# RWKV time mix: the 16-column inverse fed through a DRAM buffer instead of constant products, two units in one walk

## The chip, the cores and the metric

One core of a Trainium2 chip runs the whole program in one launch. The metric is the device time in microseconds, from a few executions of the same program; less is better. TensorE runs its matmuls in fp32 here; VectorE, ScalarE and the DMA queues of SyncE, ScalarE and GpSimd work beside it, held in order by semaphores.

## The reference

The model has four layers of width 1024 over 256 tokens, batch 1. Each layer is FFN, mixer, FFN. The mixers are RWKV-7 time mix, Mamba-2, sliding attention and RWKV-7 again; then one more block with a recurrent unit and attention follows. The change is inside the two RWKV-7 time mixes only:

```python
def step(state, inp):
    r_t, w_t, k_t, v_t, kk_t, a_t = inp
    sa = einsum('bhvk,bhk->bhv', state, -kk_t)
    state = state * w_t + sa[..., None] * (kk_t * a_t) + v_t[..., None] * k_t
    return state, einsum('bhvk,bhk->bhv', state, r_t)
```

The kernel does not step through tokens. It takes chunks of 128 tokens and writes the recurrence as products of matrices. For that, each head and chunk needs the inverse of a unit lower triangular 128x128 matrix, 1 + L, where L comes from products of the scaled `a` and `kk` (the "near" products). The inverse starts with its 16x16 diagonal blocks, which are found column by column (the "walk"), and is then grown to 32, 64 and 128 by products.

## The kernel before

There are 16 heads, laid out two to a tile of 128 partitions (eight tiles), and two chunks. A unit is one chunk (`b`) of eight heads (`hf`), `u = 2 b + hf`, so there are `UNITS = 4` units; `i` is the head's half of the partitions. `j` is 0 or 1 for the first and second RWKV sublayer (`n = 1` and `n = 10`).

TensorE's order is written out by hand in `rw_products`. It projects key tiles k0 to k7 (with the low ranks between), r0 to r7, v0 to v7, for `j = 1` the low rank v1, then g1 (two tiles), and then the second steps v2 and g2. A tile is eight products of 128x128 weights with 256 columns of a mix, into one of three PSUM banks in turn (`RING = 3`); a tile may begin when ScalarE has evacuated the tile three before it. Weights come in slots of 24 blocks (1.5 MB), three slots resident; SyncE's queue refills a slot when TensorE is done with it. The function `beside` of a tile is called after its fourth and its eighth product: there `near(u, i)` and `spread(u, i)` are placed, in r3 to r7 and v0 to v6.

The path of one unit before the change, for each half `i`: four near products (64 rows of contraction) of TensorE go to bank 3. VectorE (`base` in `rw_vector`) multiplies them with the constant `near`, which keeps the 16x16 diagonal blocks above the diagonal (L2344), sums over the eight blocks to 64 columns (L2349), and expands them with `same_row` to 1024 columns (L2352). TensorE multiplies this with the constant `same16` (`spread`, two products of 512 columns), which copies each row of a block to all of its 16 partitions, in banks 4 to 7. Then the walk: 15 pairs of VectorE instructions, a product (L2364, reading the PSUM) and a subtraction (L2365), on 8 heads and 15, 14, ... 1 columns, each waiting for the one before. The result is in `wkv_base`, read later by `open_y` (L2428). So VectorE walks four times a stage; between them it does the mixes of v and g (L2235), the bonus (L2376), `scaled_both` (L2382, L2383) and, for `j = 0`, the streamed sum of the conditioning weights (`beside`, L521: one 768 KB chunk `ada_in`, whose buffer GpSimd's queue then refills).

ScalarE (`rw_act`) evacuates every tile in TensorE's order (L2095), stores `v_first` for `j = 0` (L2133) and loads it for `j = 1` (L2137), and reads the second steps only when `scaled_both` is done (`rw_keys`). The low rank tiles v1 and g1 go to `lora`, in the arena from 8 K words on.

## Time and profile before

| what | us |
|---|---|
| three executions | 3020.34, 3021.47, 3025.54 |
| median | 3021.47 |
| span of the profiled execution, first to last instruction | 3017.6 |
| around the span, against the median | 3.9 |

The page of the profile gives for the span the busy time of each engine, a row of 40 slices, the DMA queues, the chain that ended last, the costliest groups by line, and the DMA issues. TensorE's granted clock is full in nearly all of the span (mean 0.992). No time of its own is recorded for the profiled execution beside its span, so the sums below are made against the span and carried over to the median. The timelines list merged instructions in order, with the idle time of the engine before one and what released it. An fp32 product shows as two or more records of TensorE.

### The profile page before, as it was taken

To read this page: it belongs to the slowest core of one execution; us is meant where nothing else is said; L and a number is where in the kernel's file an instruction comes from. 1 tells how busy PE (TensorE), PEld (TensorE's weight loads), DVE (VectorE), ACT (ScalarE), POOL (GpSimd) and SP (SyncE) were. 2 spreads that over 40 slices of the span, in tenths; PEclk is the share of its full clock that TensorE was granted. 3 is DMA by queue.
4 is the path that set the end of the run, shared out by engine and by line. 5 is a ranking of instruction groups with operands and counts; after the bars stand their busy time and mean duration, and the time that the engine had idled before them with its cause. 6 is when DMAs were issued, how large, how long until landed. Compare 5 with 4: busy or idle time off the path is not lost. (4 is left out here: it accounts for less than half of the span.)

```text
span 3017.6 us, 50256 instructions
## 1 busy us (share of the span) xinstructions
PE 2933.6 (97%) x20094; PEld 2574.1 (85%) x20094; DVE 2351.2 (78%) x3516; ACT 1392.3 (46%) x2260; POOL 97.2 (3%) x187
## 2 busy tenths in 40 slices
PE   7999999999999999999999999999999999999998
PEld 6887788888889888888886888887788888989887
DVE  6988877998878857888867888887865866665785
ACT  4534123555545734555444555544123544465553
POOL 0000000000000000000000000000000000000000
PEclk9999999999999999999999999999999999999999
DMA  8683436686666337666764666672303553444453
GB/s 354 256 318 147 153 105 238 249 319 229 241 241 231 112 120 271 231 256 248 270 250 157 236 253 265 237 276 84 119 23 115 200 188 127 168 149 148 171 190 133
DMA packets 69675, 609.33 MB, mean 202 GB/s; under 512 B 7728, under 2 KB 7888, under 8 KB 31824
## 3 DMA queue, kind: packets, MB, share of 16 engines
q1 hardware_dynamic: 42768, 459.36, 40.9%
q0 software_dynamic: 26352, 144.74, 12.8%
q8 instruction: 160, 2.62, 0.3%
q10 hardware_dynamic: 336, 2.13, 0.2%
q14 instruction: 59, 0.48, 0.0%
HBM read 604.10 MB, written 2.10 MB: 201 GB/s over the span
## 5 line engine op out<-in xcount | busy, mean ns | idle before, releaser
L1073 ACT ACTIVATE unit_high<-weights 128x1024 fp32r<-128x1024 f32 x576 | 609.6, 1060 | 624.9 <-PE psum L1142 335.3
L1084 DVE TENSOR_TENSOR unit_low<-weights,unit_high 128x1024 fp32r<-128x1024 f32 x576 | 703.1, 1222 | 146.9 <-ACT unit_high L1073 146.6
L1138 PE MATMUL psum<-h_part,unit_high 128*128 128x512 f32 x3024 | 769.2, 393 | 5.0 <-DVE h_part L995 5.0
L1138 PEld LDWEIGHTS psum<-h_part,unit_high 128*128 128x128 f32 x3024 | 542.0, 189 | 105.0 <-DVE h_part L995 5.5
L1142 PEld LDWEIGHTS psum<-h_part,unit_low 128*128 128x128 f32 x3024 | 416.6, 190 | 31.0
L1142 PE MATMUL psum<-h_part,unit_low 128*128 128x256 f32 x3024 | 432.3, 282 | 0.0
L331 PE MATMUL psum<-in_part,w_part 128*128 128x256 f32 x2784 | 359.4, 288 | 11.6 <-DVE in_part L999 5.8
L331 PEld LDWEIGHTS psum<-in_part,w_part 128*128 128x128 f32 x2784 | 344.7, 194 | 29.5 <-issue 15.0
L1159 PE MATMUL psum<-hidden,unit_high 128*128 128x512 f32 x1386 | 348.3, 392 | 0.0
L521 DVE SCALAR_TENSOR_TENSOR ada_sum<-ada_in,c_act,ada_sum 128x1536 f32<-128x1536 f32 x154 | 278.7, 1812 | 28.9 <-DMA ada_in<-in_ada_w 28.8
L1279 DVE TENSOR_REDUCE arena<-psum 128x256 f32<-128x512 f32 x378 | 259.9, 687 | 49.2 <-PE psum L1142 38.6
L1159 PEld LDWEIGHTS psum<-hidden,unit_high 128*128 128x128 f32 x1386 | 248.8, 189 | 44.0
L331 PE MATMUL psum<-arena,weights 128*128 128x256 f32 (+4 forms) x1360 | 270.3, 370 | 6.2 <-DVE arena L2235 4.4
L331 PEld LDWEIGHTS psum<-arena,weights 128*128 128x128 f32 (+3 forms) x1360 | 214.5, 188 | 59.0 <-issue 28.0
L1437 DVE TENSOR_TENSOR w_part<-weights,w_part 128x1024 fp32r<-128x1024 f32 x144 | 175.1, 1220 | 86.4 <-ACT w_part L1431 85.4
L1166 PEld LDWEIGHTS psum<-hidden,unit_low 128*128 128x128 f32 x1584 | 214.5, 191 | 13.3
L1166 PE MATMUL psum<-hidden,unit_low 128*128 128x256 f32 x1584 | 221.1, 282 | 0.0
L331 PE MATMUL psum<-arena 64*64 64x64 f32 (+5 forms) x2752 | 182.5, 250 | 4.1 <-DVE arena L2959 2.3
L331 PEld LDWEIGHTS psum<-arena 64*64 64x64 f32 (+3 forms) x2752 | 150.2, 148 | 31.9 <-issue 16.9
L1431 ACT ACTIVATE w_part<-weights 128x1024 fp32r<-128x1024 f32 x144 | 150.8, 1050 | 16.0 <-PE psum L331 16.0
L1244 ACT ACTIVATE hidden<-arena 128x256 fp32r<-128x256 f32 x198 | 82.9, 419 | 111.8 <-DVE arena L1346 91.0
L505 POOL DMA_DIRECT2D ada_in<-in_ada_w x130 | 68.7, 528 | 1431.2 <-DVE ada_sum L521 1090.0
(332 smaller groups left out, 2861.4 us busy)
## 6 DMA issues: line engine op xcount, KB each, us to landing
weights<-in_weights SPq DMA_DIRECT2D x290, 1536.0 KB, 6.5
ada_in<-in_ada_w POOLq DMA_DIRECT2D x182, 768.0 KB, 5.9
consts<-in_consts POOLq DMA_DIRECT2D x1, 1556.0 KB, 12.2
x<-in_x SPq DMA_DIRECT2D x1, 1024.0 KB, 8.8
v_first<-arena ACTq DMA_DIRECT2D x1, 1024.0 KB, 5.3
arena<-v_first ACTq DMA_DIRECT2D x1, 1024.0 KB, 4.8
weights<-in_weights SPq DMA_DIRECT2D x1, 512.0 KB, 5.5
out<-x SPq DMA_DIRECT2D x1, 512.0 KB, 2.7
```

Of the source, the lines that this page charges most:

```text
L331: ins = self.k.nc.tensor.matmul(out, lhsT=w, rhs=x, start=start, stop=stop, is_transpose=turn)
L521: ins = k.nc.vector.scalar_tensor_tensor(out, buf, c, out, ALU.mult, ALU.add)
L1073: k.nc.scalar.activation(k.unit_part[0][:, n % UNIT_RING], w, ACT.Copy).then_inc(k.sem["unit_high"], 1)
L1084: k.nc.vector.tensor_tensor(k.unit_part[1][:, n % UNIT_RING], w, k.unit_part[0][:, n % UNIT_RING].bitcast(FP32), ALU.subtract).then_inc(k. ...
L1138: mm(k.psum[:, 2 * (j % 2) + half, :].rearrange("p (i t) -> p i t", i=2), lhsT=part(2 * j + half, 0, t), rhs=k.h_parts[:, :, t], start=t = ...
L1142: ins = mm(k.psum[:, 2 * (j % 2) + half, 0:T], lhsT=part(2 * j + half, 1, t), rhs=k.h_part[0][:, t], start=False, stop=t == KT - 1, skip_g ...
L1159: mm(k.psum[:, out_bank(d), :].rearrange("p (i t) -> p i t", i=2), lhsT=w, rhs=x, start=f == 0, stop=f == FT - 1, skip_group_check=True)
L1166: ins = mm(k.psum[:, out_bank(d), 0:T], lhsT=part(UNITS_UP + v, 1, b), rhs=k.hidden_part[f][:, 0], start=False, stop=f == FT - 1, skip_gro ...
L1244: k.nc.scalar.activation(k.hidden_part[j][:, 0], k.hidden[:, j % RING], ACT.Copy)\
L1279: v.tensor_reduce(to[:, j % RING], k.psum[:, 2 * (j % 2) + half, :].rearrange("p (i t) -> p t i", i=2), AX.X, ALU.add).then_inc(k.sem["gat ...
L1431: self.k.nc.scalar.activation(self.k.w_part[0][:, m % RING], w, ACT.Copy).then_inc(self.k.sem["w_high"], 1)
L1437: self.k.nc.vector.tensor_tensor(self.k.w_part[1][:, m % RING], self.weights(m)[1], self.k.w_part[0][:, m % RING].bitcast(FP32), ALU.subtr ...
```

## The change

The 16x16 blocks are no longer spread by a product. `near(u)` issues the near products of both halves in one go, alternating between them, into two banks of 4 to 7; near(0) and near(1) stand within r3, near(2) and near(3) within r4. ScalarE copies only the 32x32 diagonal squares (`near_read`), VectorE picks of each the 16 columns that belong to the partition (`choose`, two instructions with the constant `halves16`). ScalarE's queue writes two units of that, 128 KB, to the DRAM buffer `near_rows` (`near_out`), and reads it back so that each partition holds all 16 rows of its block (`low_in`: two transfers of 1 MB a pair of units, each row of 8 KB going to 16 partitions) to the arena at 8 K and at 27 K words. The second place is the buffer `raw`, which was a tensor of its own and is now the arena's end, so that one access pattern with a step of 19 K words reaches both. The walk then takes two units at once, reading these instead of the PSUM. The first place is also that of `lora`, so ScalarE waits for the second walk before it reads v1 and g1. Its second `low_in` stands after the evacuation of v0 and waits for the first walk. The waits of TensorE on `wk_base` go.

```diff
-        self.step = k.small[:, 192:312]
+        self.step = k.small[:, 192:432]
-        self.spread = cut(26, 1024).rearrange("p (n s t) -> p n s t", n=4, s=16)
+        self.near_q = [cut(26 + i / 4, 256).rearrange("p (m t) -> p m t", m=8) for i in range(2)]
+        self.near_t = cut(26.5, 512).rearrange("p (u m t) -> p u m t", u=UNITS, m=8)
+    def low(k, at, *steps):
+        pitch = 27 * 1024 + KT * (T + 1)
+        return bass.AP(tensor=k.arena, offset=8 * 1024 + at, ap=[[pitch, P], *steps])
+    def low_rows(k, i):
+        pitch = 27 * 1024 + KT * (T + 1)
+        return bass.AP(tensor=k.arena, offset=(8, 27)[i] * 1024, ap=[[pitch, P], [1, 2048]])
...
-    def spread(u, i):
-        pe.wait_ge(s["wk_expanded"], 2 * UNITS * j + 2 * u + i + 1)
-        if u and i == 0:
-            pe.wait_ge(s["wk_base"], UNITS * j + u)
-        for h in range(2):
-            mm(k.psum[:, (6, 4)[i] + h, :], k.const("same16"),
-               z.spread[:, 2 * h:2 * h + 2].rearrange("p n s t -> p (n s t)"), True, True,
-               s["wk_spread"] if h else None)
+    def near(u):
+        b, hf = divmod(u, 2)
+        pe.wait_ge(s["rw_keys"], 3 * j + 1 + b)
+        if b:
+            pe.wait_ge(s["wk_near_read"], UNITS * j + u - 1)
+        for p in range(4):
+            for i in range(2):
+                mm(k.psum[:, 5 + 2 * hf - i, p * P:(p + 1) * P], z.a[z.rows(i), 4 * hf + p, z.now(b)],
+                   z.kk[z.rows(i), 4 * hf + p, z.now(b)], True, True, s["wk_near"] if p == 3 and i else None)
...
         if at == (3, 0):
-            near(0, 0)
-        if at == (3, 1):
-            near(0, 1)
+            near(0)
+            near(1)
         if at == (4, 0):
-            spread(0, 0)
...
+            near(2)
+            near(3)
...
+    def near_read(u):
+        act.wait_ge(s["wk_near"], 2 * UNITS * j + u + 1)
+        if u >= 2:
+            act.wait_ge(s["near_chosen"], UNITS * j + u - 1)
+        for g in range(4):
+            part = slice(32 * g, 32 * g + 32)
+            ps = k.psum[part, 4 + 2 * (u % 2):6 + 2 * (u % 2), :].rearrange("p i (n c) -> p i n c", n=4)
+            ins = act_(z.near_q[u % 2][part].rearrange("p (i n) c -> p i n c", i=2), ps[:, :, :, part], f.Copy)
+        ins.then_inc(s["wk_near_read"], 1)
+    def near_out(b):
+        act.wait_ge(s["near_chosen"], UNITS * j + 2 * b + 2)
+        act.dma_start(near_rows[2 * b:2 * b + 2].rearrange("u p x -> p u x"), z.near_t[:, 2 * b:2 * b + 2].rearrange("p u m t -> p u (m t)"))\
+            .then_inc(s["near_out"], 16)
+    def low_in(b):
+        if b:
+            act.wait_ge(s["wk_base"], 2 * j + 1)
+        act.wait_ge(s["near_out"], 16 * (2 * j + b + 1))
+        for i in range(2):
+            rows = near_rows[2 * b + i].rearrange("(c s) x -> c (s x)", s=16)
+            act.dma_start(z.low_rows(k, i), rows.unsqueeze(1).to_broadcast([8, 16, 16 * P])).then_inc(s["low_in"], 16)
...
+        if m == 3:
+            near_read(0)
+            near_read(1)
         evacuate("r", m, z.r[:, m], f.Copy)
+        if m == 3:
+            near_out(0)
+            near_read(2)
+            near_read(3)
+        if m == 4:
+            low_in(0)
+        if m == 5:
+            near_out(1)
     act.wait_ge(s["rw_keys"], 3 * j + 1)
     for m in range(KT):
         evacuate("v", m, z.v[:, m], f.Copy)
+        if m == 0:
+            low_in(1)
+    act.wait_ge(s["wk_base"], 2 * j + 2)
...
+    def choose(u):
+        dve.wait_ge(s["wk_near_read"], UNITS * j + u + 1)
+        even, odd = (k.const("halves16")[:, i:i + 1] for i in range(2))
+        q = z.near_q[u % 2]
+        own.of(v.tensor_scalar(z.near_t[:, u], q[:, :, 0:16], even, None, mult))
+        v.scalar_tensor_tensor(z.near_t[:, u], q[:, :, 16:32], odd, z.near_t[:, u], mult, add)\
+            .then_inc(s["near_chosen"], 1)
+
+    def base(b):
+        x = z.base[:, 2 * b:2 * b + 2]
+        own.of(v.tensor_copy(x.rearrange("p u m t -> p (u m) t"),
+                             k.const("same_row").unsqueeze(1).to_broadcast([P, 16, 16])))
+        dve.wait_ge(s["low_in"], 32 * (2 * j + b + 1))
         for c in range(15):
             w = 15 - c
-            step = z.step[:, 0:8 * w].rearrange("p (m c) -> p m c", m=8)
-            own.of(v.tensor_tensor(step, low[:, :, c, c + 1:16], x[:, :, c:c + 1].to_broadcast([P, 8, w]), mult))
-            own.of(v.tensor_tensor(x[:, :, c + 1:16], x[:, :, c + 1:16], step, sub))
+            step = z.step[:, 0:16 * w].rearrange("p (u m c) -> p u m c", u=2, m=8)
+            low = z.low(k, c * P + c + 1, [19 * 1024, 2], [16, 8], [1, w])
+            own.of(v.tensor_tensor(step, low, x[:, :, :, c:c + 1].to_broadcast([P, 2, 8, w]), mult))
+            own.of(v.tensor_tensor(x[:, :, :, c + 1:16], x[:, :, :, c + 1:16], step, sub))
...
-    base(0, value_mixes, lambda: None)
-    base(1, lambda: None, gate_mixes)
-    base(2, beside, bonus)
-    base(3, beside, scaled_both)
+    choose(0)
+    choose(1)
+    value_mixes()
+    choose(2)
+    choose(3)
+    beside(2)
+    base(0)
+    gate_mixes()
+    bonus()
     beside()
+    base(1)
+    scaled_both()
```

## Rows read from the trace of the kernel before

**Rows 1.** The page, part 1: busy us, share of the span, instructions.

```profile
PE 2933.6 (97%) x20094; PEld 2574.1 (85%) x20094; DVE 2351.2 (78%) x3516; ACT 1392.3 (46%) x2260; POOL 97.2 (3%) x187
```

**Rows 2.** Busy time by stretch: us, PE, PEld, DVE, ACT, POOL, clock, DMA share, GB/s.

```profile
291.40:369.50 78.10, 75.11 (x329) 56.92 (x328) 68.73 (x181) 7.03 (x16) 1.06 (x2) 1.00 0.35 129
2102.70:2182.20 79.50, 78.04 (x345) 60.12 (x344) 65.50 (x180) 7.41 (x17) 0.00 (x0) 1.00 0.31 115
```

**Rows 3.** Timeline of TensorE, stage A: start us, us, engine line op, [idle before <-releaser].

```profile
291.43 1.16 PE L331 MATMUL psum<-arena 64*128 64x128 f32 x8
292.51 1.99 PE L331 MATMUL psum<-arena,weights 128*128 128x256 f32 x8
...
301.47 1.88 PE L331 MATMUL psum<-arena,consts 128*128 128x512 f32 x4
303.18 1.89 PE L331 MATMUL psum<-arena,weights 128*128 128x256 f32 x8
...
369.51 5.21 PE L331 MATMUL psum<-arena,weights 128*128 128x256 f32 x32 [0.47 <-ACT arena L2095]
```

**Rows 4.** Timeline of TensorE, stage B.

```profile
2102.75 1.16 PE L331 MATMUL psum<-arena 64*128 64x128 f32 x8
...
2182.24 3.71 PE L331 MATMUL psum<-arena,weights 32*128 32x256 f32 x32 [0.47 <-ACT arena L2095]
...
2189.38 1.16 PE L331 MATMUL psum<-arena 64*128 64x128 f32 x16
2190.47 3.72 PE L331 MATMUL psum<-arena,consts 128*128 128x256 f32 x16
```

**Rows 5.** Timeline of VectorE, stage A.

```profile
303.45 0.28 DVE L2364 TENSOR_TENSOR small<-psum,wkv_base 128x120 f32<-128x120 f32 x1 [2.08 <-PE psum L331]
303.77 0.28 DVE L2365 TENSOR_TENSOR wkv_base<-wkv_base,small 128x120 f32<-128x120 f32 x1
...
311.01 0.17 DVE L2365 TENSOR_TENSOR wkv_base<-wkv_base,small 128x8 f32<-128x8 f32 x1
311.22 0.15 DVE L2366 COPY small<-consts 128x1 f32<-128x1 f32 x1
311.29 0.68 DVE L2344 TENSOR_TENSOR arena<-psum,consts 128x512 f32<-128x512 f32 x1
...
314.20 0.68 DVE L2344 TENSOR_TENSOR arena<-psum,consts 128x512 f32<-128x512 f32 x1
...
337.61 3.25 DVE L2376 SCALAR_TENSOR_TENSOR arena<-arena,params 128x256 f32<-128x256 f32 x8
...
358.82 2.28 DVE L2383 TENSOR_TENSOR arena<-arena 128x2048 f32<-128x2048 f32 x1
...
369.06 1.82 DVE L521 SCALAR_TENSOR_TENSOR ada_sum<-ada_in,c_act,ada_sum 128x1536 f32<-128x1536 f32 x1
```

**Rows 6.** Timeline of ScalarE, stage A.

```profile
308.12 0.38 ACT L2095 ACTIVATE arena<-psum 128x256 f32<-128x256 f32 x1 [6.07 <-PE psum L331]
311.57 0.38 ACT L2095 ACTIVATE arena<-psum 128x256 f32<-128x256 f32 x1 [3.07 <-PE psum L331]
...
362.96 1.28 ACT L2095 ACT_TABLE_LOAD   x1 [0.41 <-ACT arena L2095]
...
372.23 1.21 ACT L2095 ACTIVATE arena<-psum 128x256 f32<-128x256 f32 x4 [2.77 <-PE psum L331]
```

**Rows 7.** The page, part 6: DMA issues, KB each, median us to landing.

```profile
out<-x SPq DMA_DIRECT2D x1, 512.0 KB, 2.7
```

**Rows 8.** DMA issues of the stretch 2100 to 2185 us.

```profile
weights<-in_weights SPq DMA_DIRECT2D x5, 1536.0 KB, 6.2
arena<-v_first ACTq DMA_DIRECT2D x1, 1024.0 KB, 4.8
```

**Rows 9.** Busy time by stretch, two slices of stage A.

```profile
303.30:305.40 2.10, 2.10 (x12) 1.61 (x11) 1.74 (x7) 0.00 (x0) 0.00 (x0) 1.00 0.50 80
...
307.50:309.60 2.10, 2.10 (x11) 1.87 (x10) 1.79 (x10) 0.38 (x1) 0.00 (x0) 1.00 0.85 363
```

More of the change, by code:

```diff
@@ L216, in const_parts @@
         "head_ones": same,
-        "same16": row // 16 == col // 16,
-        "near": (row // 16 == col // 16) & (row < col),
+        "halves16": row[:, 0:1] // 16 % 2 == np.arange(2)[None, :],
         "same_row": row % 16 == np.arange(16)[None, :],
@@ L423, in layout @@
     k.wkv_base = sb("wkv_base", [P, 512])
[L424 removed]
+    k.raw = k.arena[:, 27 * 1024:].rearrange("p (n t) -> p n t", n=KT)
     k.raw_bias = k.small[:, 488:490]
@@ L451, in layout @@
               "rw_turned_read", "rw_gated", "v_first_moved",
-              "wk_near", "wk_expanded", "wk_spread", "wk_base", "wk_am", "wk_open", "wk_y",
+              "wk_near", "near_chosen", "near_out", "low_in", "wk_base", "wk_am", "wk_open", "wk_y",
               "wk_x_read", "wk_lx", "wk_t", "wk_x32", "wk_x32_read", "wk_y32",
@@ L1782, in rw_products @@
     for m in range(KT):
-        tile("v", m, 4, beside_v)
+        tile("v", m, 4)
     if j:
@@ L1795, in rw_products @@
     evacuated("g1", 1)
-    pe.wait_ge(s["wk_near_read"], 2 * UNITS * (j + 1))
+    pe.wait_ge(s["wk_near_read"], UNITS * (j + 1))
     for i in range(2):
@@ L2081, in norm_bank, with rw_act @@
     return 5 if n == 0 or n < NORMS and SUBS[n - 1] != "ffn" else 3
-def rw_act(k, act, ev, j, v_first):
+def rw_act(k, act, ev, j, v_first, near_rows):
     s, z, f, tiles = k.sem, RwTiles(k), ACT, RwOrder(j, ev.q)
@@ L2165, in at, with near_again_read @@
         act.wait_ge(s[name], c.count(step, steps))
-    def near_read(c):
-        act.wait_ge(s["wk_near"], 3 * UNITS * j + 2 * UNITS + c.u + 1)
+    def near_again_read(c):
+        act.wait_ge(s["wk_near"], 2 * UNITS * j + UNITS + c.u + 1)
         act_(z.am[c.hf], c.pair(0), f.Copy).then_inc(s["wk_am"], 1)
@@ L2209, in rw_act @@
         if n < UNITS:
-            near_read(units[n])
+            near_again_read(units[n])
         if n >= 2:
@@ L2284, in rw_vector @@
         mod_columns(k, dve, own, n + 1)
-    v.tensor_scalar(z.one_less_ka, k.param(f"rw_k_a{j}", 0, KT), -1.0, 1.0, mult, add).then_inc(s["rw_one_less"], 1)
+    own.mark(v.tensor_scalar(z.one_less_ka, k.param(f"rw_k_a{j}", 0, KT), -1.0, 1.0, mult, add))
     beside(2)
@@ L2293, in scaled_key @@
         return v.tensor_tensor(z.k[:, t], z.k[:, t], z.k_factor[:, t], mult)
-    dve.wait_ge(s["rw_one_less"], j + 1)
+    own.wait()
     for t in range(KT):
@@ L2339, in value_mixes @@
             mix(4, t)
-    def base(u, lead, between):
-        for i in range(2):
-            dve.wait_ge(s["wk_near"], 3 * UNITS * j + 2 * u + i + 1)
-            v.tensor_tensor(z.near, k.psum[:, 3, :].rearrange("p (n t) -> p n t", n=4),
-                            k.const("near").unsqueeze(1).to_broadcast([P, 4, P]), mult).then_inc(s["wk_near_read"], 1)
-            if i == 0:
-                lead()
-            dve.wait_ge(s["wk_near_read"], 2 * UNITS * j + 2 * u + i + 1)
-            own.of(v.tensor_reduce(z.near_t, z.near.rearrange("p n (c t) -> p n t c", t=16), AX.X, add))
-            if i:
-                dve.wait_ge(s["wk_spread"], 2 * UNITS * j + 2 * u + 1)
-            v.tensor_tensor(z.spread, z.near_t.unsqueeze(2).to_broadcast([P, 4, 16, 16]),
-                            k.const("same_row").unsqueeze(1).unsqueeze(3).to_broadcast([P, 4, 16, 16]), mult)\
-                .then_inc(s["wk_expanded"], 1)
-        x = z.base[:, u]
-        own.mark(v.tensor_copy(x, k.const("same_row").unsqueeze(1).to_broadcast([P, 8, 16])))
-        between()
-        own.wait()
-        dve.wait_ge(s["wk_spread"], 2 * UNITS * j + 2 * u + 2)
-        low = k.acc.rearrange("p t (s c) -> p t s c", s=16)
@@ L3856, in build @@
     v_first = nc.dram_tensor("v_first", (P, KT, T), FP32, kind="Internal").ap()
+    near_rows = nc.dram_tensor("near_rows", (UNITS, P, P), FP32, kind="Internal").ap()
     with ctx:
@@ L3898, in _ @@
                 elif kind == "rwkv":
-                    rw_act(k, act, ev, n, v_first)
+                    rw_act(k, act, ev, n, v_first, near_rows)
                 elif kind == "mamba":
```

49 lines of the change are left out of this document (4 added, 45 removed).

## The prediction

> **What bounds the kernel now.** I read the busy shares first: TensorE is busy for 97% of the span, no other engine for more than 78% [rows 1]. So the question for any edit is what it does to TensorE's order, and for work that leaves TensorE the question is who becomes late instead. The change sits in two stages, the "r", "v" and "g1" projections of the two RWKV sublayers. Their windows are 291.4 to 369.5 and 2102.7 to 2182.2 us, and TensorE is busy for 75 of 78 and 78 of 80 us there at full clock, with VectorE at 69 and 66 [rows 2]. I call the first stage A and the second B. In TensorE's own timeline [rows 3, 4] the reader sees three kinds of work in turn: projections (sixteen records a tile), a near product (8 records, 64 rows) and a spread (4 records, 512 columns). TensorE is idle for 3.0 us of A and 1.5 of B in all, 0.47 of it right before "g2" [rows 2 to 4]. So it carries these stages; VectorE is nearly as full, and starts what follows its last walk at 369.06, half a microsecond before "g2" [rows 3, 5]. Outside them both orders stay, and behind them TensorE is again the busy engine, so I take time saved there as kept.
>
> **Part 1, the spread goes.** Each stage has 8 spreads (4 units, two halves). From the start of one to the start of the next work is 303.18 - 301.47 = 1.71 us [rows 3]. 8 x 1.71 = 13.7 us a stage.
>
> **Part 2, near products by pairs.** Now 8 groups of 8 records at 1.08 us (292.51 - 291.43) [rows 3]. The new loop alternates the two 64-row halves, which is how the near products are taken again later: 16 records in 2190.47 - 2189.38 = 1.09 us [rows 4]. So four groups of 1.09 instead of eight of 1.08: 4.3 us less a stage.
>
> **TensorE's new stage.** A tile of sixteen records takes 3.45 us (ScalarE's evacuations at 308.12 and 311.57) [rows 6]. A holds 14.5 tiles from 291.43 on (half of r3, r4 to r7, eight v, two g1), B one more (v1). A: 14.5 x 3.45 = 50.0, near 4.4, two changes to 64 rows and back 0.4, last wait 0.5, together 55.3 instead of 369.51 - 291.43 = 78.1: 22.8 less. B: 15.5 x 3.45 = 53.5 + 5.3 = 58.8 instead of 79.5: 20.7 less. Parts 1 and 2 are 18.0 of it; the rest are the waits on VectorE and some changes between shapes. If nothing else is late, 43.5 us go, and "g2" starts at 346.7 and 2161.5.
>
> **Part 3, VectorE.** Masking, reducing and expanding go (one half takes 314.20 - 311.29 = 2.9 us, 8 a stage: 23 us), replaced by eight products of 128 columns. A product of 120 columns takes 0.28 us [rows 5]; I take 0.3, some 2.4 us. One walk takes 311.22 - 303.45 = 7.8 us. A step of 120 columns takes 0.28 us and one of 8 takes 0.17, which is 1 ns a column [rows 5]; the doubled walk adds 2 x 960 columns = 2.0 us, so 9.8 us for two units instead of 15.5. Its operand now comes from SBUF with a stride; L2364 (from PSUM) and L2365 (SBUF only) both take 0.28 us, so I charge nothing for that, and up to 5.8 us (two separate walks) as the other bound. The Trainium skill's page VectorE: DVE Perf Modes, section on the TRN2 errata, has a table in which a PSUM source costs 62 cycles more than an SBUF source. By it, an estimate, each walk's fifteen reads would be 1 us shorter; the two lines of the walk show no such difference. VectorE is then free for more than half of the stage, so it isn't the bound by its own work.
>
> **Part 4, ScalarE.** Sixteen copies of 256 columns on 32 partitions a stage, by the copies of 128x256: 0.38 alone, 0.30 in a row of four [rows 6], so 1.2 to 1.5 us a unit, hidden: ScalarE is busy for 7 us of the stage [rows 2]. What isn't hidden is its order. The low_in of block 1 waits for walk 0 (the buffers are reused), and behind it on ScalarE stand the evacuations of v1 to v7. TensorE has three banks, so tile v4 waits for v1. After v7, ScalarE waits for walk 1 before it evacuates g1 (and v1's low rank), and "g2" on TensorE waits for g1.
>
> **Part 5, the way through DRAM: the unknown.** One near_out writes 128 KB. The nearest rows are a store of 512 KB (2.7 us) and a load of 1 MB (4.8) [rows 7, 8]; issued at 296, it lands by 299 or by 301, before ScalarE has done r4 (301.8), so it costs nothing at either end. One low_in is two transfers of 1 MB each on ScalarE's queue. Call its time from issue to landing L. 1 MB in the v_first load takes 4.8 us, a 1.5 MB slot 6.2 [rows 8]; the difference is 2.8 us a MB, leaving 2.0 fixed, and the engines move 363 GB/s at a share of 0.85 [rows 9], 427 at full. At that rate two MB take 4.9 us, so L is at least 6.9, alone and over all engines. But v_first has 128 rows on each side, and low_in's source has eight rows of 8 KB in front, each sent to sixteen partitions. No row here shows how such a transfer is dealt out. If only eight of the sixteen engines get it, the data take 9.8 us and L is 11.8 alone. I take this, as the rows in front are what can be dealt out and the whole megabyte comes from 64 KB of DRAM; that choice is the weakest step. The Trainium skill's page DMA: Bandwidth & Descriptors (section "Why a DMA increments its semaphore by 16 and not by 1") says that the number of engines is the largest up to 16 that divides the slowest dimension of both sides, which is 8 here, and its rules for kernel authors warn of a short outermost dimension. No row of this case shows such a transfer.
>
> Others share those engines. A slot of 1.5 MB is 3.7 us of each engine at that rate, an ada_in of 0.75 MB 1.8. A slot is freed at the start of r5, its data begin some 2 us later (80 GB/s in the slice from 303.3 on [rows 9], where r5 began at 303.18 [rows 3]), and in the new order r5 starts at 301.4, at the moment of low_in 0. The next slot comes with v0, ten us later. In A beside(2) also frees two ada_in at 303 and 305.
>
> **Sum, stage A.** low_in 0 issued 301.8. L = 2.0 + 9.8 + 3.7 (slot) + 3.7 (two ada_in) + 3.7 (next slot) = 22.9, landed 324.7; walk to 334.5. TensorE could start v4 at 325.5; it starts at 335.6 (issue of low_in 1, v1's evacuation). low_in 1 issued 335.2; L = 11.8 + 3.7 + part of one ada_in = 16; gate mixes and bonus (3.25 us each) and one ada product (1.82) [rows 5] hide in it. Walk 351.2 to 361.0. Then v_first's issue, the table load (1.28) and two evacuations [rows 6]: "g2" at 363.5, 6.0 before today. **Stage B** lies 1811.3 later and has no ada_in. low_in 0 issued 2113.1, L = 11.8 + 3.7 + 2.5 = 18, walk ends 2140.9; low_in 1 issued 2141.6, L = 15.5, walk ends 2166.9; "g2" at 2169.8, 12.4 before today. scaled_both (two products of 2.28 us [rows 5]) ends behind the walk but ahead of its users, because TensorE has 5 us of "g2" products first. Together 18.4 us.
>
> **Rivals.** (a) The transfers run over all engines. A: L0 = 2.0 + 4.9 + 3.7 + 3.7 = 14.3, walk to 325.9, v4 at 327.0, 1.5 late; the rest on time. B on time. 43.5 - 1.5 = 42 us: 2979.5. For it: every transfer in the trace with 128 rows in front; against it: the shape. (b) The stalls are heavier than my shares: each L is 2 to 4 us more, or each walk is by a stride that costs as much: 8 to 16 us of the gain, 3011 to 3019. (c) Slower. "g2" in A starts at 324.6 + L0 + L1, so the sign turns at L0 + L1 = 44.9 (45.9 in B), a mean of 22.7. It needs low_in at a quarter of the engines, or slowed by reading the same DRAM row sixteen times: data 19.6 instead of 9.8, four times 9.8 more, 39 - 18 = 21 us slower: 3042. (d) The halved near groups or the merged walk bring less than their rows say, as TensorE's gain is covered by the DRAM path anyway: no change of the result unless (a) holds, then 2984.
>
> **Numbers.** Before: span 3017.6, median of the runs 3021.5, so 3.9 lie around the span and stay. 3021.5 - 18.4 = 3003. Chances: forecast 0.55, (a) with (d) 0.28, (b) 0.12, (c) 0.05. The range runs from 2978 (all 43.5) to 3013 (each L 2.5 us more). Within 0.2% (6 us, about what a measurement of this kernel can tell from no change) is part of (b). Faster 0.88, same 0.07, slower 0.05.
>
> **What would show it.** TensorE: no 512-column products on consts in these windows, near groups of 16 records at 1.09. VectorE: steps of 240 columns at 0.41 us. ScalarE's DMA rows: low_in's time to landing, 12 to 23 us by the forecast, 7 to 14 by (a). TensorE idle before v4 and before "g2", released by ScalarE: 10 and 6 us in A, 5 and 3 in B; under 3 in all by (a). If L is below 12 everywhere, the forecast is wrong by its weakest step. If there is idle time elsewhere, the assumption that saved time is kept is wrong.

## The result and the profile after

| | median of the runs, us | lowest to highest | profiled execution's span | mean granted clock |
|---|---|---|---|---|
| before | 3023.16 (4 runs, one more beside the changed kernel) | 3020.34 to 3025.54 | 3017.6 | 0.992 |
| after | 3061.44 (4 runs) | 3060.17 to 3064.65 | 3060.0 | 0.978 |

The ratio is 1.0133, with a 95% interval of 1.0121 to 1.0145: the changed kernel is 38 us slower. The forecast was 3003, with a range of 2978 to 3013, so the size and the sign were both wrong.

TensorE's timeline of stage A in the changed kernel (start, us, and the idle time before it with its releaser) answers to [rows 3]:

```profile
293.36 2.06 PE L330 MATMUL psum<-arena 64*128 64x128 f32 x32
...
299.00 2.06 PE L330 MATMUL psum<-arena 64*128 64x128 f32 x32
300.98 26.17 PE L330 MATMUL psum<-arena,weights 128*128 128x256 f32 x120
354.21 23.23 PE L330 MATMUL psum<-arena,weights 128*128 128x256 f32 x96 [27.06 <-ACT arena L2061]
395.32 7.32 PE L330 MATMUL psum<-arena,weights 128*128 128x256 f32 x32 [17.88 <-ACT arena L2061]
402.57 1.16 PE L330 MATMUL psum<-arena 64*128 64x128 f32 x16
```

and of stage B, which answers to [rows 4]:

```profile
2132.61 2.06 PE L330 MATMUL psum<-arena 64*128 64x128 f32 x32
...
2140.24 26.17 PE L330 MATMUL psum<-arena,weights 128*128 128x256 f32 x120
2189.27 27.33 PE L330 MATMUL psum<-arena,weights 128*128 128x256 f32 x112 [22.87 <-ACT arena L2061]
2224.51 6.00 PE L330 MATMUL psum<-arena,weights 32*128 32x256 f32 x32 [7.91 <-ACT arena L2061]
```

The order of work is the one forecast: near products in two short groups, no products with a constant, then projections without a gap up to v4. The two stalls stand where the prediction put them, before v4 and before "g2", both released by ScalarE. Only their size is another: 27.1 and 17.9 us in A (10 and 6 forecast), 22.9 and 7.9 in B (5 and 3 forecast). From the first near product to the end of "g2" the stage grew by 26.0 us in A (402.57 - 293.36 = 109.2 us, 83.2 before) and by 14.7 in B. That is 40.7 us, where the runs differ by 38.3 and the two profiled spans by 42.4; ahead of A, between the stages and behind B the spans differ by 2 us or so each, so nothing of size changed there.

Why ScalarE was late is read on VectorE and on ScalarE's queue. These are the first rows of both walks and the issues of low_in in stage A, then VectorE in stage B:

```profile
342.53 0.41 DVE L2361 TENSOR_TENSOR small<-arena,wkv_base 128x240 f32<-128x240 f32 x1 [34.86 <-DMA arena<-near_rows]
382.96 0.41 DVE L2361 TENSOR_TENSOR small<-arena,wkv_base 128x240 f32<-128x240 f32 x1 [22.21 <-DMA arena<-near_rows]
```

```profile
303.02 1.17 ACTq L2088 DMA_DIRECT2D arena<-near_rows  x1
304.23 0.59 ACTq L2088 DMA_DIRECT2D arena<-near_rows  x1
...
352.52 1.21 ACTq L2088 DMA_DIRECT2D arena<-near_rows  x2
353.77 0.94 ACT L2061 ACTIVATE arena<-psum 128x256 f32<-128x256 f32 x3 [36.50 <-issue]
```

```profile
2177.59 0.41 DVE L2361 TENSOR_TENSOR small<-arena,wkv_base 128x240 f32<-128x240 f32 x1 [34.13 <-DMA arena<-near_rows]
2212.11 0.41 DVE L2361 TENSOR_TENSOR small<-arena,wkv_base 128x240 f32<-128x240 f32 x1 [18.02 <-DMA arena<-near_rows]
```

VectorE stood still for the transfer, four times. From the issue to the first step of the walk, L is 342.53 - 303.02 = 39.5 and 382.96 - 352.52 = 30.4 us in A. In B low_in is issued at 2142.27 and 2187.58, so L is 35.3 and 24.5. The forecast had 22.9, 16, 18 and 15.5. The four differences add up to 57.4 us, and the forecast missed by 3061.4 - 3003 = 58.4 (56.7 in the change, 18.4 less forecast and 38.3 more measured). That these come so close is partly chance, since slower records of TensorE, below, add 4.4 us to the stages that no L holds.

Two more views show what the transfer did and suffered. The page's queue of ScalarE (packets, MB, share of 16 engines), and the DMA issues of the stretch 290 to 400 us (KB each, median us to landing):

```profile
q10 hardware_dynamic: 2512, 11.04, 1.3%
```

```profile
weights<-in_weights SPq DMA_DIRECT2D x5, 1536.0 KB, 16.9
...
ada_in<-in_ada_w POOLq DMA_DIRECT2D x3, 768.0 KB, 20.4
```

The queue has 2512 packets, where it had 336. The 2176 more are 8 x 136 for the low_in and 4 x 272 for the stores. 136 is 128 rows of 8 KB and 8 small packets. I read the small ones as one for each engine that took part: eight of the sixteen. A transfer with 128 rows in front has 144 packets, 16 small ones (run 1, below). And a weight slot, which landed in 6.8 us in stage A before (median of the stretch 290 to 370 us) and in 6.2 in B [rows 8], now took a median of 16.9 in A and 14.7 in B. In A without any low_in (run 2) it takes 6.2.

### The profile page after: what moved, and what is told of

It reads as the page before. It is cut to its first block and busy times, and to the rows that moved or that the text cites. A ratio compares the mean times of both kernels' runs of the same rounds, so it can differ in the third digit from the quotient of the medians.

```text
span 3060.0 us, 50004 instructions
## 1 busy us (share of the span) xinstructions
PE 2906.1 (95%) x20030; PEld 2564.7 (84%) x20030; DVE 2292.3 (75%) x3356; ACT 1403.5 (46%) x2292; POOL 97.2 (3%) x187
## 3 DMA queue, kind: packets, MB, share of 16 engines
q10 hardware_dynamic: 2512, 11.04, 1.3%
## 5 line engine op out<-in xcount | busy, mean ns | idle before, releaser
L330 PEld LDWEIGHTS psum<-in_part,w_part 128*128 128x128 f32 x2784 | 345.7, 194 | 30.0 <-issue 15.5
L330 PE MATMUL psum<-arena,weights 128*128 128x256 f32 (+4 forms) x1360 | 276.4, 382 | 80.8 <-ACT arena L2061 76.6
L330 PEld LDWEIGHTS psum<-arena,weights 128*128 128x128 f32 (+3 forms) x1360 | 223.0, 195 | 130.5 <-ACT arena L2061 78.6
L330 PE MATMUL psum<-arena 64*64 64x64 f32 (+5 forms) x2752 | 172.2, 250 | 2.9 <-DVE arena L2963 2.3
L330 PEld LDWEIGHTS psum<-arena 64*64 64x64 f32 (+3 forms) x2752 | 142.3, 148 | 26.5 <-issue 15.6
```

What stands on the lines that cost most here:

```text
L330: ins = self.k.nc.tensor.matmul(out, lhsT=w, rhs=x, start=start, stop=stop, is_transpose=turn)
```

## What was tried, and what each run showed

Three theories of the long L: **E**, the transfer runs on eight engines, as I had taken, and the rest of L is work of other queues beside it; **R**, on top of that the same DRAM row is read sixteen times; **P**, on top of E the destination, sixteen neighbouring partitions for each row in front, slows the packets. Single executions below have no interval; the beginning of stage A alone lay anywhere from 291.4 to 296.8 us between kernels, so differences under 5 us between single runs are not read. The kernel before took 3024.5 and 3025.4 beside the first two groups of runs.

**1. The transfers alone.** No part of the kernel; each transfer of 1 MB is issued when the one before has landed:

```python
("rows128", [[ROW, 128]]), ("eight_repeated", [[ROW, 8], [0, 16]]),
("eight_distinct", [[17 * ROW, 8], [ROW, 16]]), ("sixteen_repeated", [[ROW, 16], [0, 8]]), ("one_row", [[0, 128]])
```

> Leaves out all of the model's computation: it only times transfers of 1 MB (128 rows of 8 KB) from DRAM to SBUF on ScalarE's queue, each alone, each case twice. The changed kernel's low_in took 39 and 30 us in the first stage. Theory E (eight engines, the rest is other traffic): with eight source rows in front, rows repeated or not, 1 MB lands in about 7 us, with 128 or sixteen rows in front in about 4.5, repetition makes no difference, and the pair of low_in alone takes 12, beside a weight slot on SyncE's queue 15. Theory R (the repeated read of one DRAM row is slow): eight distinct is at most 7, but eight repeated, sixteen repeated and one row are far above it, the pair alone at 20 or more.

The start of one issue to the start of the next is the time of a transfer (ScalarE's queue in its timeline):

```profile
7.98 0.35 ACTq L77 DMA_DIRECT2D d_rows<-in_w  x1
12.90 1.16 ACTq L77 DMA_DIRECT2D d_eight_repeated<-in_w  x1
23.67 0.61 ACTq L77 DMA_DIRECT2D d_eight_distinct<-in_w  x1
34.83 0.59 ACTq L77 DMA_DIRECT2D d_sixteen_repeated<-in_w  x1
41.79 0.33 ACTq L77 DMA_DIRECT2D d_one_row<-in_w  x1
46.21 1.23 ACTq L77 DMA_DIRECT2D pair<-near_rows  x2
67.15 0.81 ACTq L77 DMA_DIRECT2D pair<-in_w  x2
74.52 1.21 ACTq L77 DMA_DIRECT2D pair<-near_rows  x2
```

128 rows: 4.9 us. Eight in front: 10.8 with repeated rows and 11.2 with distinct ones. Sixteen in front: 7.0. One single row, read 128 times: 4.4. The pair of low_in with nothing beside it: 67.15 - 46.21 = 20.9, where I had 11.8; a pair of 128-row loads: 7.4. Beside one weight slot the pair took 24.5 us, and 23.1 the second time. R falls: repetition costs nothing. E alone falls too. This is how 128 rows and eight in front move (length, GpSimd's busy time, clock, share of 16 engines, GB/s):

```profile
7.98:12.90 4.92, 0.00 (x0) 1.00 0.61 213
12.90:23.67 10.77, 0.00 (x0) 1.00 0.39 97
```

The share times the length is how long all sixteen engines would be busy with the megabyte. For 128 rows it is 0.61 x 4.92 = 3.0 us; an engine has 8 packets of 8 KB, 0.38 us each. For eight in front it is 0.39 x 10.77 = 4.2 us of sixteen engines, so 8.4 of eight, for 16 packets each, 0.53 us a packet. (The packet counts of the two are 144 and 136.) So the packets themselves are 1.4 times as long, and there are twice as many to an engine.

**2. No low_in at all.** The walk reads the constants instead; nothing waits for DRAM.

```diff
-        for i in range(2):
-            rows = near_rows[2 * b + i].rearrange("(c s) x -> c (s x)", s=16)
-            act.dma_start(z.low_rows(k, i), ...).then_inc(s["low_in"], 16)
...
-        dve.wait_ge(s["low_in"], 32 * (2 * j + b + 1))
...
-            low = z.low(k, c * P + c + 1, [19 * 1024, 2], [16, 8], [1, w])
+            low = bass.AP(tensor=k.consts, offset=CONST_AT["ident"][0] + c + 1, ap=[[CONSTS, P], [16, 2], [8, 8], [1, w]])
```

> The changed kernel without low_in: nothing is read back from near_rows, and the walk takes its operand from a constant. By the sum of the prediction TensorE's stages are then 55.3 and 58.8 us, no wait for ScalarE, clock full: 43.5 us less than before, about 2979. If more than the transfers holds the stages (ScalarE's order, the walk, the write to DRAM), it is above 2985.

2980.2 us, a single execution, 44.3 under the kernel before beside it. TensorE in stage A:

```profile
292.67 2.06 PE L330 MATMUL psum<-arena 64*128 64x128 f32 x32
...
300.29 46.89 PE L330 MATMUL psum<-arena,weights 128*128 128x256 f32 x216
347.65 2.64 PE L330 MATMUL psum<-arena,weights 128*128 128x256 f32 x16 [0.47 <-ACT arena L2061]
```

The stage is 347.65 - 292.67 = 55.0 us (55.3 forecast), in B 2142.32 - 2083.89 = 58.4 (58.8 forecast), and all of the gain arrives at the end (44 us, 43.5 forecast). The same group of TensorE in part 5 of the page or the answer by lines (count, busy and mean ns, idle before, releasers), first of this kernel and then of the changed one:

```profile
L330 PE MATMUL psum<-arena,weights 128*128 128x256 f32 (+4 forms) x1360 | 265.5, 370 | 6.2 <-DVE arena L2235 4.4 <-ACT arena L2061 1.8
```

```profile
L330 PE MATMUL psum<-arena,weights 128*128 128x256 f32 (+4 forms) x1360 | 276.4, 382 | 80.8 <-ACT arena L2061 76.6 <-DVE arena L2238 4.3
```

76.6 - 1.8 = 74.8 us of waiting for ScalarE and 276.4 - 265.5 = 10.9 us of slower records. Together they are 85.7, against 81.2 us between the two kernels; where the other 4 us come back I did not find.

**3. Other shapes of the same transfer in the kernel.** e_distinct128 loads 128 rows of the weights instead, e_distinct8b eight in front and 16 distinct rows of the weights behind each, e_sixteen writes two copies of each matrix to DRAM and puts 16 rows in front:

```diff
-        act.dma_start(near_rows[2 * b:2 * b + 2].rearrange("u p x -> p u x"), ...)\
-            .then_inc(s["near_out"], 16)
+        for h in range(2):
+            for i in range(2):
+                act.dma_start(near_rows[2 * b + i, :, h], z.near_t[:, 2 * b + i].rearrange("p m t -> p (m t)"))\
+                    .then_inc(s["near_out"], 16)
...
-            rows = near_rows[2 * b + i].rearrange("(c s) x -> c (s x)", s=16)
-            act.dma_start(z.low_rows(k, i), rows.unsqueeze(1).to_broadcast([8, 16, 16 * P]))...
+            rows = near_rows[2 * b + i].rearrange("c h s x -> (c h) (s x)")
+            act.dma_start(z.low_rows(k, i), rows.unsqueeze(1).to_broadcast([16, 8, 16 * P]))...
```

> low_in reads 128 distinct rows of 8 KB from the weights in DRAM instead of near_rows (the same bytes to the same places, other data): output wrong. Both theories: L as rival (a), 7 to 14 us, time about 2980 to 2985. If L stays above 20, neither the shape nor the repetition is the cause, but the traffic beside it.

> The changed kernel with low_in reading 128 distinct rows of the weights, but with eight rows in front and sixteen behind each (output wrong). Repetition alone differs from the changed kernel. Theories E and P: same time as the changed kernel, 3058 to 3064. Theory R: faster by 10 us or more.

> near_out writes every block of rows twice, so that low_in's source has sixteen rows in front, each read eight times. Theory E: low_in about halves, 18 us and less, time about 2985 to 3000. Theory R: the repeated read stays and little is gained, above 3040.

| low_in in | L0, L1 in A, us | TensorE idle before v4, "g2" in A | time, us |
|---|---|---|---|
| 8 in front, repeated (changed kernel) | 39.5, 30.4 | 27.1, 17.9 | 3061.4 |
| 8 in front, distinct (e_distinct8b) | 40.5, 29.4 | 28.1, 17.5 | 3060.7 |
| 16 in front, repeated (e_sixteen) | 18.5, 12.6 | 7.3, 0.5 | 2989.7 |
| 128 in front, distinct (e_distinct128) | 12.6, 10.0 | none, 0.5 | 2979.5 |

The first step of walk 0 in e_distinct128 and the row of TensorE that runs through v4 without a stop:

```profile
314.27 0.41 DVE L2360 TENSOR_TENSOR small<-arena,wkv_base 128x240 f32<-128x240 f32 x1 [7.99 <-DMA arena<-in_weights]
```

```profile
299.61 47.04 PE L330 MATMUL psum<-arena,weights 128*128 128x256 f32 x216
```

The last three rows are single executions. Between the second row and the last the number of bytes, the tensor they come from, their places and the waits are the same and the shape is another, and the kernel moves by 81 us. Repetition again costs nothing. So the shape of low_in is the cause of the loss, shown in the kernel itself. The last row is also rival (a) of the prediction, whose sum gave 2979.5.

**4. Shapes, alone again.** Two studies of single transfers of 1 MB with distinct rows, to find what makes a packet long, and the pair of low_in beside three weight slots. The first:

> Leaves out all of the model's computation: transfers of 1 MB alone, each case twice, all from distinct DRAM rows, differing in how many rows stand in front and how many neighbouring partitions follow on each; then a store of sixteen copies (1 MB); then the changed kernel's pair of low_in beside three weight slots. Theory E (count of engines alone; eight are slower than half for a reason of their own): eight by 4 partitions as eight by 16, 11 us; sixteen by 4 as sixteen by 8, 7. Theory P (besides the count, neighbouring partitions share a way into SBUF, and engines that go through their partitions in step meet there): eight by 4 touches 32 partitions, one group of four an engine, 7 us instead of 11, though it has the same engines; sixteen by 8 stays at 7, 128 rows in front at 4.9. The pair beside three slots takes 32 to 39 by both, as in the kernel.

The store of that run, two of 1 MB one after the other, took 3.9 us each and is not used here. The second, with its controls (one row for each of fewer partitions; groups of 2, 4 and 8; eight transfers of 16 rows):

> Transfers alone, one after the other, each with its own rows of DRAM and 1 MB long (one of 512 KB), twice over; nothing of the kernel is computed. Controls that were missing: 64 and 32 rows of 16 and 32 KB (one partition each), eight groups of 8 and of 16 partitions, sixteen groups of 8 and of 2, thirty-two of 2, sixteen of 4 at 8 KB a partition (512 KB), and 1 MB as eight transfers of 16 rows, each the same row of DRAM sixteen times. Theory P (engines that run in step write into neighbouring groups at the same place and get in each other's way): one partition per row is fast whatever the number of partitions, 5 to 5.5 us; groups of 2 too; the half megabyte by groups of 4 takes 3.6 to 4.8; the eight transfers of 16 rows run on all engines, no two at the same place of a group, and take 6.5 to 7.5 (issue 0.6 us each). Rival B (what is slow is a large number of bytes in one partition, or few partitions, not the grouping): 64 rows of 16 KB take 7.5 as the groups of 4 did, 32 rows of 32 KB 7.5 to 11. Rival L (what is slow is a long run of transfers on one engine under one row in front): eight transfers of 16 are fast, and one partition per row is fast, but groups of 2 at 32 KB are as slow as groups of 8, 7.5.

Some rows of the second's ScalarE queue:

```profile
5.76 0.34 ACTq L59 DMA_DIRECT2D d_rows_all<-in_w  x1
10.59 0.54 ACTq L59 DMA_DIRECT2D d_rows_sixtyfour<-in_w  x1
18.29 0.35 ACTq L59 DMA_DIRECT2D d_rows_thirtytwo<-in_w  x1
25.42 1.14 ACTq L59 DMA_DIRECT2D d_eight_bysixteen<-in_w  x1
36.95 0.61 ACTq L59 DMA_DIRECT2D d_eight_byeight<-in_w  x1
49.10 0.59 ACTq L59 DMA_DIRECT2D d_sixteen_byeight<-in_w  x1
...
77.34 3.62 ACTq L56 DMA_DIRECT2D d_split<-in_w  x8
87.46 0.35 ACTq L59 DMA_DIRECT2D d_rows_all<-in_w  x1
```

The last column is again share times length, the time for which all sixteen engines would be busy with the megabyte. The engines are counted by the small packets.

| rows in front x partitions behind each, KB a partition | engines | 1 MB, us (with those of run 1) | us of sixteen engines |
|---|---|---|---|
| 128 x 1, 8 | 16 | 4.8 to 5.2 | 2.9 to 3.0 |
| 64 x 2, 8 | 16 | 5.3 | 3.0 |
| 32 x 4, 8 | 16 | 5.2 | 3.0 |
| 16 x 8, 8 | 16 | 6.8 to 7.6 | 4.5 to 4.7 |
| 16 x 4, 16 | 16 | 7.6 | 4.6 |
| 64 x 1, 16 | 16 | 7.7 | 4.7 |
| 32 x 1, 32 | 16 | 7.1 | 4.8 |
| 32 x 2, 16; 16 x 2, 32 | 16 | 7.8; 8.2 | 4.7; 4.9 |
| 8 x 4, 32 | 8 | 7.8 | 2.9 |
| 8 x 16, 8 | 8 | 10.8 to 11.5 | 4.2 to 4.5 |
| 8 x 8, 16 | 8 | 12.2 | 4.7 |
| eight transfers of 16 rows, one DRAM row each | 16 | 10.1 | 7.8 |

The last row of the table comes from this line (length, GpSimd, clock, share, GB/s):

```profile
77.34:87.46 10.12, 0.00 (x0) 1.00 0.77 104
```

The pair of low_in beside three slots is in the first study. It was issued at 114.72, and the next issue on ScalarE's queue is at 148.43, but that one waited for the third slot too. All 2 x 136 packets of the pair began before 144 us:

```profile
q10 hardware_dynamic: 272, 2.10, 29.7%
```

(ScalarE's queue in the stretch 114.7 to 144 us; the last packet began at 143.7). So the pair took some 29 us, 8 more than alone, and 3.58 of the three slots' 4.72 MB moved meanwhile, 2.3 slots: 3.6 us a slot, where I had 3.7. The pair beside one slot in run 1 agrees, with 3.6 and 2.1 us more than alone. The range of 32 to 39 us that both theories gave was missed.

P fits the first study and not the second: 64 rows with one partition each are as slow as 16 groups of 8, so grouping isn't what makes a packet long; and eight transfers of 16 rows, on all engines, are slow as well. The rival of bytes in a partition fits these, but not 8 x 4 with 32 KB, whose packets aren't long: 0.37 x 7.76 us of sixteen engines is 2.9 us a MB, as the 128 rows take. What all runs show is this: the full rate came at 8 KB a partition over all 128 partitions with 32 or more rows in front, and every departure from it cost 2 to 7 us a MB. The last column adds that the engines' work for a megabyte came in three sizes, 2.9 to 3.0, 4.2 to 4.9 and 7.8 us, and that eight in front by 16 is in the middle one, as sixteen in front by 8 is; the rest of its time comes from having half the engines. Which property of the shape sets a packet's length stays open. It need not be the destination's: the length and the spacing of the source's rows changed along with it in these studies and were not varied alone.

**5. A later place for the waits.** e_late2 is e_sixteen with the second low_in behind v3's evacuation instead of v0's; e_order2 is e_late2 with the first low_in ahead of r4's evacuation.

```diff
-        if m == 0:
+        if m == 3:
             low_in(1)
```

> Two copies as before (sixteen rows in front), and ScalarE issues low_in 1 after the evacuation of v3 instead of v0. If TensorE's wait before v4 cost time by itself, its 7 us in the first stage come back: 2983. If the chain through DRAM sets the start of g2, the wait only moves there: 2988 to 2990.

> As the run before, and low_in 0 is issued before r4's evacuation instead of behind it, 1.6 us earlier in each stage. If the chain sets g2, 1.6 us less in the first stage and up to that in the second: 2985 to 2987. If not, no change.

2998.0 and 3007.7 us in single executions, no better than e_sixteen (2989.7, and 2998.8 as the median of run 6) and above what either alternative said. In e_late2 the stall before v4 is gone, and stands before "g2":

```profile
362.54 7.21 PE L330 MATMUL psum<-arena,weights 128*128 128x256 f32 x32 [16.54 <-ACT arena L2061]
```

So the chain through DRAM sets the end of the stage, and where ScalarE waits for it only moves the stall. From the first near product to "g2" stage A is even 6.7 us longer than in e_sixteen, because TensorE, running on, frees weight slots whose loads then lie beside the second low_in: two slots are issued and 2.10 MB of them move during it, none in e_sixteen, and L1 is 17.9 us here and 12.6 there. In e_order2 the same happens (L1 19.8, idle time of 18.7 us before "g2"), and the earlier first low_in brings nothing, with an L0 of 20.6.

**6. Versions that could beat the kernel before.** e_sixteen was timed again; e_thirtytwo writes four copies (eight stores of 64 KB for two units) and puts 32 rows in front.

> The kernel of e_sixteen once more, now timed beside the kernel before in alternating rounds, so that its gain has an interval. From its one execution (2989.7 us against 3024.5): 0.9885, 2986 to 2994 us. Under the rival that its single time was a lucky one (the stage's start varied by 3 to 5 us between executions): 2993 to 2998 us.

> Four copies of each unit's matrix are written to DRAM (eight stores of 64 KB for two units instead of four), so that low_in has 32 rows in front and 4 neighbouring partitions for each. Everything is computed. Theory P (neighbouring partitions share a way into SBUF, beside the engine count): the transfers alone took 5.2 us for 1 MB in this form against 7.5 with 16 in front, so a pair is some 4 to 5 us shorter than in e_sixteen, the first wait (18.5 us there) becomes 13 to 15.5, the stall of 7.3 us before v4 becomes 2 to 5 and the stall of 3.7 us in the second layer goes; 2979 to 2986 us. Theory E (the number of engines alone, 16 in both): the waits stay at 16 to 19 us, the four more stores add 2 to 3 us, and the time is 2990 to 2994 us.

> e_thirtytwo with the second unit pair's eight stores moved from behind r5's evacuation to behind v0's, just ahead of low_in(1). Everything is computed. Cause tested: in e_thirtytwo those stores took 13.8 us to issue on ScalarE, because they stood on its queue behind low_in(0)'s 2 MB, and r6 and the tiles behind it waited for their evacuation (9.4 us of TensorE in the first layer, 0.6 in the second). By that cause the 9.4 us go; what stays is the wait of v4 for ScalarE, which stands at the walk's end behind v0: with low_in(0) issued at 310 and some 13 us long the walk ends at 333, v4's natural place is 326, so 6 to 8 us of stall stay, 5 to 8 us less than the mean of e_thirtytwo's two stalls and slower records: 2984 to 2989 us. If the long issue came from the stores themselves (eight of them wherever they stand), v1's evacuation is as late as r6's was and the time stays at 2990 to 2994 us.

> e_thirtytwo_b with low_in(1) moved from behind v0's evacuation to behind v2's, so that v1 and v2 are evacuated before ScalarE waits for the walk's end, and TensorE stops at v6, not v4. Everything is computed. Theory of the chain (the longest path is near rows, store, low_in(0), walk 0, low_in(1), walk 1, g2): walk 1 ends where it did, at 353 to 357 us of the first layer, and g2's natural place is 348 to 350, so the stall moves to g2 and stays at 4 to 8 us: within 0.1% of e_thirtytwo_b. Rival (the place at which ScalarE waits is the cost): the stall before v4 goes with nothing in its place, and the time is 5 to 8 us under e_thirtytwo_b's.

The edit of e_thirtytwo_c against e_thirtytwo:

```diff
-        if m == 5:
-            near_out(1)
...
         if m == 0:
+            near_out(1)
+        if m == 2:
             low_in(1)
```

| | ratio to before | 95% interval | idle before the v tiles, A and B, us |
|---|---|---|---|
| e_sixteen_timed | 0.9917 | 0.9900 to 0.9933 | 8.6, 4.2 |
| e_thirtytwo | 0.9895 | 0.9878 to 0.9911 | 9.4, 0.6 |
| e_thirtytwo_b | 0.9904 | 0.9888 to 0.9921 | 11.6, 0.5 |
| e_thirtytwo_c | 0.9885 | 0.9868 to 0.9901 | 4.4, none |

All four beat the kernel before, by 24 to 33 us between the medians. e_sixteen's single execution was a lucky one: its median is 2998.8, just above the 2993 to 2998 of the rival. ScalarE's queue in stage A of e_thirtytwo:

```profile
298.21 6.32 ACTq L2081 DMA_DIRECT2D near_rows<-arena  x8
...
310.35 1.25 ACTq L2090 DMA_DIRECT2D arena<-near_rows  x2
...
311.67 13.82 ACTq L2081 DMA_DIRECT2D near_rows<-arena  x8
325.54 0.94 ACT L2061 ACTIVATE arena<-psum 128x256 f32<-128x256 f32 x3 [13.51 <-issue]
```

L0 is 15.4 us in A, as I had expected (325.75 - 310.35), and 11.0 in B, against 18.5 and 16.2 in e_sixteen, so the shape does what the transfers alone said. The time, 2992, is nevertheless in the range of the other theory, for another reason: the eight stores take 6.3 us to issue, so the first low_in leaves at 310 instead of 303, and the next eight, behind 2 MB on the same queue, take 13.8 (7.1 in B). Moving them behind v0 (e_thirtytwo_b) leaves 9.7 of the 13.8 and gains nothing, where I had 5 to 8 us: the walk's end is what v4 waits for. Moving the second low_in as well (e_thirtytwo_c) removes most of the idle time, and the median is 4.7 us under e_thirtytwo_b's, between what the theory and the rival said. That is not a clear gain: its interval overlaps that of e_thirtytwo and just touches that of e_sixteen_timed. It is still 9 us above the single execution with no low_in (run 2). In A the trace shows 4.4 us idle before the v tiles, 1.9 before "g2" and 1.6 in slow records of "g2" (6.80 us for 5.21).

**7. The shape without a copy.** e_split issues each 1 MB as eight transfers, one for each chunk of 16 partitions; e_split_late has the second low_in behind v2.

```diff
...
+            for c in range(8):
+                row = near_rows[2 * b + i, 16 * c:16 * c + 16].rearrange("(o s) x -> o (s x)", o=1)
+                act.dma_start(z.low_rows(k, i, c), row.to_broadcast([16, 16 * P])).then_inc(s["low_in"], 16)
...
```

> The changed kernel with each 1 MB of low_in issued as eight transfers of 16 partitions, one for each chunk, whose source is one DRAM row of 8 KB sixteen times. One copy in DRAM, as in the changed kernel; everything is computed. Theory (shape): sixteen in front, so all engines, and no collision in a group: the transfers are bound by their issue, 16 of some 0.6 us, and the wait is 12 to 15 us from the first issue. ScalarE's evacuations stand behind 10 us of issues twice: r5's late (TensorE has two tiles in hand, 6.9 us, so 3 us of stall), v1's 10 us behind the walk's end. First layer: walk 0 from 316 to 326, low_in 1 until 336, v4 some 10 us late, g2 2 to 4 late; second layer the same. 2994 to 3004 us. Rival (small transfers cost more than their issue, each 2 us fixed one after the other): the waits stay at 30 us and the time at 3040 to 3060.

> e_split with low_in(1) behind v2's evacuation instead of v0's, so that v1 and v2 are out of the way before the ten us of issues. Everything is computed. If the place of ScalarE's wait is the cost, the stall before v4 goes and one of 2 to 4 us before v6 or g2 stays in each layer: 2984 to 2990 us. If the chain through DRAM sets the end, no more than 3 us under e_split.

1.0034 (1.0019 to 1.0048) and 1.0032 (1.0019 to 1.0044) of the kernel before: 1% better than the changed kernel, but slower than the kernel before. e_split is 27 us above the top of my theory and 9 below the rival's range, so neither sum held. e_split_late is within 1 us of it, as expected if the chain through DRAM sets the end; the other alternative, 2984 to 2990, falls. L0 of e_split in A is 338.65 - 302.06 = 36.6 us:

```profile
302.43 9.46 ACTq L2089 DMA_DIRECT2D arena<-near_rows  x15
...
348.63 7.38 ACTq L2089 DMA_DIRECT2D arena<-near_rows  x16
356.06 0.94 ACT L2061 ACTIVATE arena<-psum 128x256 f32<-128x256 f32 x3 [39.21 <-issue]
```

```profile
338.65 0.41 DVE L2362 TENSOR_TENSOR small<-arena,wkv_base 128x240 f32<-128x240 f32 x1 [31.94 <-DMA arena<-near_rows]
```

The issues took 9.8 and 7.4 us, where I had 10. What I had not priced is the transfers' own time. Alone, 1 MB takes 10.1 us with 3.6 us of issuing, and its packets fill 7.8 us of sixteen engines, 2.6 times as much as with 128 rows. In the kernel L0 is 36.6 in A and 22.4 in B, where there is no ada_in; how much of A's is waiting beside slots and ada_in was not measured. So "more engines" alone isn't the recipe; the form of the whole transfer counts.

## Why the prediction was wrong, step by step

- **Parts 1 and 2, TensorE's new stage: right.** 55.0 us for 55.3 in A and 58.4 for 58.8 in B, the near pairs 1.0 us each for 1.09, 44 us in all for 43.5 (run 2). Saved time was kept outside the stages, as assumed.
- **Part 3, the walk: right.** Walk 0 in A runs from 342.53 to 352.33, 9.8 us as forecast. Its steps of 240 columns take 0.41 us for both lines (above, and L2362 in the trace at 0.41), so the strided source in SBUF costs nothing. A product of 112 columns takes 0.28 us from SBUF in this trace and 0.27 from PSUM in the one before. So the extra 62 cycles of a PSUM source, in the table of the Trainium skill's page VectorE: DVE Perf Modes, section on the TRN2 errata, don't show here, and the measurement decides. The picking of columns takes 0.29 and 0.35 us a unit, 2.6 us a stage for 2.4.
- **Part 4, the order of the waits: right.** v4 waits for v1's evacuation behind low_in(1), and "g2" for walk 1. The formula of rival (c), that the sign turns at L0 + L1 = 44.9 (A) and 45.9 (B), holds with the measured L: 69.9 - 44.9 = 25.0 and 59.9 - 45.9 = 14.0 us, where the trace has 23.9 and 12.4 to the start of "g2".
- **Part 5, L: the step that failed**, in the sentence "the data take 9.8 us and L is 11.8 alone". The eight engines were right: the transfer has 136 packets, 8 of them small. The rule in the Trainium skill's page DMA: Bandwidth & Descriptors, section "Why a DMA increments its semaphore by 16 and not by 1", gives eight, and the trace agrees. But I took each engine's rate from transfers with 128 rows in front. Alone, L is 20.9, and the share of 0.44 over that time (46.21 to 67.15 us of run 1) means 18.4 us of work for each of the eight engines, where the sum had 9.8. Of the 8.6 us between them 2.2 are the rate itself, as 128 rows alone need 3.0 us of sixteen engines a MB and I had 2.45; the other 6.4 are the longer packets of this shape. 9.1 us more, four times, is 36.4 of the 57.4 us. The number of engines that the rule gives was no price of the transfer, and I took it as one.
- **The shares of other work** were right by the piece (3.6 us a slot for 3.7, run 4), but not in number: a longer window takes in more slots. L0 in B has 35.3 - 20.9 = 14.4 us beside the pair's own time, and three slots are issued in it, where I had 1.7. Three slots at 3.6 are 10.9; what the other 3.5 are stays open. More of other queues' work beside the transfers is the other 21 us of the 57.4, by subtraction; which slot cost what in the kernel was not measured.
- **The clock was missing.** The granted clock of the stages fell from 1.00 [rows 2] to 0.80 and 0.83 (length, busy PE, PEld, DVE, ACT, POOL, clock, share, GB/s):

```profile
293.30:397.30 104.00, 59.06 (x302) 50.75 (x302) 40.39 (x100) 12.72 (x32) 1.58 (x3) 0.80 0.58 156
2132.60:2226.00 93.40, 62.62 (x322) 53.44 (x322) 34.71 (x97) 13.11 (x33) 0.00 (x0) 0.83 0.56 146
```

  After each long idle time the records are slow: "g2" takes 7.32 us in A, and 5.21 in e_sixteen, whose "g2" follows 0.5 us of idle time. From 395.3 to 399.0, where TensorE is busy with it again, the granted clock is 0.50, the lower of its two levels, 1.2 of 2.4 GHz. In B it takes 6.00 against 3.71. These are 2.1 + 2.3 us, which stand on the path; the slower v tiles are covered by the wait for walk 1.
- **The rivals.** (c) had the right sign and mechanism with the wrong trigger: I tied it to a quarter of the engines or to repeated rows, neither of which is true, and gave it 0.05. Its condition, a mean L of 22.7, needed only that a transfer of unseen shape be twice as slow as the nearest row says. Its own sum, 3042, was still 19 us short. My bounds for L came from one kind of row (128 in front) on both sides.

## What to carry to other kernels

Price a DMA whose shape isn't in the trace as unknown by a factor of two to three, not by dividing bytes by engines: 1 MB took 4.4 to 12.2 us here by its shape alone. When a step leaves the busy engine for a way through DRAM, write down at which L the sign turns, as that formula held within 2 us, and give the chance of crossing it by what is known of L, which here was a guess from one kind of row. If data must be repeated into many partitions, try writing a few copies first, so that 32 or more rows stand in front and all partitions get their share; here it turned a loss of 1.3% into a gain of 1.1%, and the cost is the issues of the extra stores on the engine that issues them.

## What the runs showed of the hardware

- Reading one DRAM row of 8 KB 128 times (4.4 and 4.6 us for 1 MB) is no slower than reading 128 rows (4.9 and 4.8).
- With eight rows in front a transfer ran on eight engines (136 packets, 8 small, for 144 and 16 with 128 rows), and its packets were also longer: 0.53 us for 8 KB against 0.38 with 128 rows.
- A slow transfer slows the others: weight slots landed in 16.9 us (median, A) instead of 6.8 in the kernel before and 6.2 in the one without low_in, and the store of 128 KB behind low_in(0) on the same queue landed after 36.3 us in the stretch 303 to 342 us:

```profile
near_rows<-arena ACTq DMA_DIRECT2D x1, 128.0 KB, 36.3
```

- Eight small stores behind 2 MB on one queue held ScalarE for 13.8 us of issuing in A and 7.1 in B, where the same eight on an empty queue took 6.3 and 5.0 (e_thirtytwo). So the 2 MB ahead alone don't explain the 13.8; A has ada_in loads beside them, and whether those are the rest was not tried.
